# A first stage with the modulation weights ahead of x, and two stage ends interleaved with half output blocks

## The reference, cut to what matters

```python
def first_block(x, c, ctx, c_ctx, ada_w, ...):            # x (1,512,1024), ctx (1,256,1024)
    sh_l, sc_l, gt_l = adaln(c, ada_w[0], ada_b[0])        # silu(c) @ w + b, split in three
    h_lat = rms_norm(x, norm_g[0]) * (1 + sc_l) + sh_l
    h_ctx = rms_norm(ctx, norm_g[0]) * (1 + sc_c) + sh_c   # the same with c_ctx
    y_lat = hgrn_mixer(h_ctx, h_lat, ...)                  # 5 projections a head, scan, norm, gate, @ hg_w_out
    x = x + gt_l * y_lat
    h = rms_norm(x, norm_g[1]) * (1 + sc) + sh
    u, z = split(h @ ft_w_in, 2)
    y = real(fft2(u in 8 groups of 256 channels)) * silu(z)
    x = x + gt * (y @ ft_w_out)
    return rms_norm(x, final_g)
```

## Time and profile before

| | |
|---|---|
| three runs | 2678.82, 2682.83, 2678.87 us |
| the profiled execution | 2684.97 us, of it the span from first to last instruction 2683.3 us |
| PE matmul busy | 2537.6 us, 95% |
| DVE, ACT, POOL busy | 1622.8 (60%), 1002.2 (37%), 113.7 us (4%) |
| mean granted clock of PE | 0.978 of full |
| DMA | 223.82 MB, mean 83 GB/s |
| one cut of a block | `w_hi` on ACT 1.06 us (line 847), `w_lo` on DVE 1.22 us (line 1324), means |
| ACT, 128x512 from PSUM | 0.60 us (line 937) |

### The profile page before, as it was taken

How to read it: one execution, slowest core, us unless ns; L and a number is a source line. 1 busy time by engine, 2 the same in 40 slices (tenths; PEclk the granted TensorE clock), 3 DMA queues, 4 the chain that set the end, 5 groups by cost and what they waited for, 6 DMA issues and landing times.

```text
span 2683.3 us, 40458 instructions
## 1 busy us (share of the span) xinstructions
PE 2537.6 (95%) x14516; PEld 2181.5 (81%) x14516; DVE 1622.8 (60%) x2366; ACT 1002.2 (37%) x1350; POOL 113.7 (4%) x140
## 2 busy tenths in 40 slices
PE   6999999999999998999899999989999899999996
PEld 1788888888888776888789999978888667888885
DVE  5567777777777645444455343468999755544445
ACT  3334444444344323333244222245545443322222
POOL 0011211121111000000000000000000000000000
PEclk9999999999999998999899999989999899999998
DMA  5122221221122222222122222222222212222222
GB/s 225 63 71 66 74 71 63 70 78 63 63 70 78 86 87 69 73 70 74 60 86 94 86 94 87 93 79 89 95 92 86 77 63 86 94 94 94 94 94 86
DMA packets 59817, 223.82 MB, mean 83 GB/s; under 512 B 6496, under 2 KB 6496, under 8 KB 59264
## 3 DMA queue, kind: packets, MB, share of 16 engines
q1 hardware_dynamic: 56544, 207.94, 23.3%
q0 software_dynamic: 3232, 15.34, 1.6%
HBM read 221.15 MB, written 2.10 MB: 83 GB/s over the span
## 4 chain that ended last, share of the span: by engine, by line
PE 85%; DVE 6%; ACT 4%; issue 3%; DMA 1%; DVEq 0%; ACTq 0%; SPq 0%; POOL 0%
PE ps L441 74%; PE ps L600 4%; PE ps L622 1%; PE ps L498 1%; DVE w_lo L1324 1%; DVE cv L1927 1%; ACT L942 1%; DMA ada_raw<-in_ada_weights_dram 1%; PE ps L641 1%; PE ps L613 1%; PE ps L632 1%; PE ps L587 1%; PE ps L634 1%; PE ps L633 1%; ACT w_hi L847 0%
## 5 line engine op out<-in xcount | busy, mean ns | idle before, releaser
L847 ACT ACTIVATE w_hi<-w_raw 128x1024 fp32r<-128x1024 f32 x360 | 381.4, 1060 | 1003.7 <-PE ps L441 998.0
L1324 DVE TENSOR_TENSOR w_lo<-w_raw,w_hi 128x1024 fp32r<-128x1024 f32 x360 | 439.7, 1222 | 256.6 <-ACT w_hi L847 254.7
L441 PE MATMUL ps<-n_hi,w_hi 128*128 128x512 f32 (+1 forms) x992 | 323.9, 358 | 30.1 <-DVE w_lo L1324 16.4
L441 PE MATMUL ps<-n_hi,w_lo 128*128 128x512 f32 (+1 forms) x992 | 320.6, 355 | 0.0
L441 PE MATMUL ps<-n_lo,w_hi 128*128 128x512 f32 (+1 forms) x992 | 320.4, 355 | 0.0
L441 PE MATMUL ps<-h_hi,w_hi 128*128 128x512 f32 x640 | 273.6, 428 | 8.4 <-DVE h_lo L1351 4.2
L441 PE MATMUL ps<-h_hi,w_lo 128*128 128x512 f32 x640 | 255.3, 399 | 0.0
L441 PE MATMUL ps<-h_lo,w_hi 128*128 128x512 f32 x640 | 254.8, 398 | 0.0
L441 PEld LDWEIGHTS ps<-n_hi,w_hi 128*128 128x128 f32 x992 | 175.0, 190 | 66.5 <-issue 21.5
L441 PEld LDWEIGHTS ps<-n_lo,w_hi 128*128 128x128 f32 x992 | 176.4, 191 | 27.2 <-issue 0.2
L441 PEld LDWEIGHTS ps<-n_hi,w_lo 128*128 128x128 f32 x992 | 175.7, 190 | 26.6
(11 more groups left out here) (338 smaller groups left out, 5075.5 us busy)
## 6 DMA issues: line engine op xcount, KB each, us to landing
w_raw<-in_weights_dram SPq DMA_DIRECT2D x376, 512.0 KB, 3.3
ada_raw<-in_ada_weights_dram SPq DMA_DIRECT2D x4, 2048.0 KB, 25.8
gate_raw<-in_gate_weights_dram POOLq DMA_DIRECT2D x16, 512.0 KB, 3.6
x<-in_x_dram SPq DMA_DIRECT2D x1, 2048.0 KB, 11.1
x<-in_x_dram POOLq DMA_DIRECT2D x1, 2048.0 KB, 7.8
out_dram<-fin POOLq DMA_DIRECT2D x1, 2048.0 KB, 6.5
xc<-in_ctx_dram POOLq DMA_DIRECT2D x1, 1024.0 KB, 11.2
masks<-in_masks_dram POOLq DMA_DIRECT2D x1, 512.0 KB, 13.4
```

The costliest lines, as they stand in the source:

```text
L441: last = nc.tensor.matmul(o, w, xp, start=start and n == 0, stop=stop and n == 2)
L847: run(w_hi[:, s], w_raw[:, s], ACT.Copy).then_inc(hi_ready[s], 1)
L1324: tt(w_lo[:, s], w_raw[:, s], w_hi[:, s].bitcast(F32), ALU.subtract).then_inc(lo_ready[s], 1)
```

## The change

Three parts of the program change.

1. First stage. SP loads modulation part 0 ahead of x, and ctx after part 1; POOL issues identity after ctx has landed and the masks after part 3 has. The squares go through two buffers. The context mean is taken on PE right after modulation part 1, into bank 5. ACT rather than DVE copies the modulation rows. DVE divides x and ctx by their roots in place (`over_root`) while PE still works on the modulation; afterwards ACT makes `h_hi` straight from the divided x with scale and bias, and DVE makes a temporary and `h_lo` beside it (`first_lo`).
2. Last head. All eight half blocks of the first four outputs are taken inside the pass, in 16 parts, at every place where a projection part stood and two after the norm. The four later half blocks leave out the tiles of the last two heads (`LATE` = 2), whose weights ACT and DVE keep aside (`kept_hi`, `kept_lo`). After the pass PE adds these two heads to the four banks. DVE's four residual additions then read banks at `early_done`.
3. Last Fourier group. The stream's order is changed (`OUT_ORDER`) so that four first halves of the output come before four second halves. The first halves run between the steps of group 7, the second halves after it, with waits on the last two y tiles alone. `residual(RF)` runs the last four rows; `raw_residual` is written out rather than looped, also for its second user.

```diff
-            sp.dma_start(x0[:], x_in).then_inc(x_in_s, 16)
             for n, (dst, a, b_) in enumerate(ADA_LOADS):
                 sp.dma_start(dst, ada_in[a:b_].rearrange("b p n -> p b n")).then_inc(ada_loaded[n], 16)
-            with sp.Fori(0, nblocks // 2) as i:
+                if n == 0:
+                    sp.dma_start(x0[:], x_in).then_inc(x_in_s, 16)
+                elif n == 1:
+                    sp.dma_start(xc[:], ctx_in).then_inc(xc_in_s, 16)
+            with sp.Fori(0, BLOCKS_TO_OUT // 2) as i:
...
-            pool.dma_start(xc[:], ctx_in).then_inc(xc_in_s, 16)
+            pool.wait_ge(xc_in_s, 16)
+            pool.dma_start(ident[:], ident_in).then_inc(ident_in_s, 16)
+            pool.wait_ge(ada_loaded[3], 16)
             pool.dma_start(masks[:], mask_in).then_inc(const_in_s, 16)
-            pool.dma_start(ident[:], ident_in).then_inc(ident_in_s, 16)
...
             for n, (raw_, a, b_) in enumerate(ADA_LOADS):
-                if n == 3:
-                    mean(N0, T, st_sum[:, 0])
                 pe.wait_ge(ada_loaded[n], 16)
                 for k in range(KD):
+                    if n == 1 and k == KD - 2:
+                        mean(N0, T, st_sum[:, 0])
...
+                if n == 1:
+                    mean(N0C, TC, st_sum[:, 1], bank=5)
...
+                parts = iter([(k, n) for k in range(2 * EARLY) for n in range(2)])
+                def begin_output():
+                    k, n = next(parts)
+                    xs = as_cut({"lo": y_cut}, whole(y_hi, y_lo))
+                    if n == 0:
                         s = take(k)
                         pe.wait_ge(acc_free, HEADS * 6 + 2)
+                    at, half = k // EARLY * KD, (KD - (LATE if k >= EARLY else 0)) // 2
+                    last = tiles(k % 2, [ps[:, k % EARLY]], xs, range(at + half * n, at + half * (n + 1)),
+                                 k < EARLY and n == 0, False, half * n)
...
+            pe.wait_ge(kept_s, EARLY)
+            for n in range(LATE):
+                t = HEADS - LATE + n
+                pe.wait_ge(y_cut, t + 1)
+                for k in range(EARLY):
+                    last = three([ps[:, k]], kept_hi[:, k, n * P:(n + 1) * P], kept_lo[:, k, n * P:(n + 1) * P],
+                                 [y_hi[:, t]], [y_lo[:, t]], False, n == LATE - 1)
+                    if n == LATE - 1:
+                        last.then_inc(early_done, 1)
...
-                project(0); turn(); project(1); over_tokens(0); over_tokens(1)
-                project(2); over_channels(0); project(3); over_channels(1)
+                project(0); turn(); project(1); begin_output(0); over_tokens(0); begin_output(1); over_tokens(1)
+                project(2); begin_output(2); over_channels(0); project(3); begin_output(3); over_channels(1)
...
-            residual(RF, KD // 2, 2, whole(y_hi, y_lo), T)
+            st.enter(0, EARLY)
+            for k in range(EARLY):
+                s = take(k)
+                tiles(s, [ps[:, k]], last_y, range(KD, 2 * KD), False, True).then_inc(w_used[s], 1)
+            st.leave(1)
+            residual(RF, (KD - EARLY) // 2, 2, whole(y_hi, y_lo), T, done=EARLY)
...
+            def over_root(N, x, rt_):
+                dve.wait_ge(N["root"], 1)
+                own.link(v.reciprocal(rt_, rt_))
+                for k in range(KD):
+                    tt(x[:, k], x[:, k], rt_, ALU.mult).then_inc(N["tmp"], 1)
+            over_root(N0, x0, st_sq[:])
             cut(0)
             cut(1)
+            over_root(N0C, xc, st_tmpc[:, 2])
...
+            def first_lo(N, x, n, tmp, hi, lo):
+                for k in range(KD + 1):
+                    if k < KD:
+                        if k > 1:
+                            dve.wait_ge(N["lo"], k - 1)
+                        own.mark(ts(tmp(k), x[:, k], scale[:, n, k:k + 1], ada0[:, k, n:n + 1], ALU.mult, ALU.add))
+                    if k:
+                        own.wait(1 if k < KD else 0)
+                        dve.wait_ge(N["hi"], k)
+                        tt(lo(k - 1), tmp(k - 1), hi(k - 1).bitcast(F32), ALU.subtract).then_inc(N["lo"], 1)
...
+                def early_after(k):
+                    if i is not None:
+                        return
+                    if EARLY <= k + 2 < 2 * EARLY:
+                        s, use = st.slot(k + 2)
+                        dve.wait_ge(kept_s, k + 3 - EARLY)
+                        tt(kept_lo[:, k + 2 - EARLY], w_raw[:, s, BLK - LATE * P:BLK],
+                           kept_hi[:, k + 2 - EARLY].bitcast(F32), ALU.subtract)
+                    cut(k + 2)
```

More of the change, by code:

```diff
@@ L53 @@
 Z_BANK = 2
+BLOCKS_TO_OUT = HEADS * 6 + 2 * KD + 4 * GROUPS
+OUT_ORDER = [BLOCKS_TO_OUT + 2 * m + n for n in range(2) for m in range(EARLY)]
+LATE = 2
 EPS = 1e-6
@@ L201, in program @@
         h_hi, h_lo = h.take("h_hi", [P, KD, T], F32R), h.take("h_lo", [P, KD, T], F32R)
+        kept = h.over()
+        kept_hi, kept_lo = [kept.take(f"kept_{n}", [P, EARLY, LATE * P], F32R) for n in ("hi", "lo")]
         hc_hi, hc_lo = h.take("hc_hi", [P, KD, TC], F32R), h.take("hc_lo", [P, KD, TC], F32R)
@@ L479, in mean @@
                 else:
-                    last = nc.tensor.matmul(ps[:, 6, 0:n], ones_d[:], src[:, 0:n], start=True, stop=True)
+                    last = nc.tensor.matmul(ps[:, bank, 0:n], ones_d[:], src[:, 0:n], start=True, stop=True)
                 last.then_inc(N["mean"], 1)
@@ L506, in _ @@
             last.then_inc(ada_done, 1)
-            pe.wait_ge(N0["root"], 1)
-            mean(N0C, TC, st_sum[:, 1])
+            pe.wait_ge(N0C["root"], 1)
             def tile(t):
@@ L913, in dve @@
                     act.wait_ge(dve_scan, j * DVE_SCAN + n)
+                def early_after(k):
+                    if i is not None or j is None:
+                        return
+                    st.wait_done(act, k)
+                    if EARLY <= k + 2 < 2 * EARLY:
+                        s, use = st.slot(k + 2)
+                        act.wait_ge(w_loaded[s], use * 16 + 16)
+                        run(kept_hi[:, k + 2 - EARLY], w_raw[:, s, BLK - LATE * P:BLK], ACT.Copy).then_inc(kept_s, 1)
+                    cut(k + 2)
                 def refill(k):
                     if i is None:
-                        if j is not None and k < EARLY:
-                            after(k)
-                    elif k == 3:
+                        return
+                    if k == 3:
                         s, _ = st.slot(5)
@@ L1136, in _, with raw_residual @@
             st.leave(GROUPS - 1)
+            st.enter(0, EARLY)
             act_group(None, GROUPS - 1)
[L1139 to L1152, removed]
+            st.leave(1)
+            def raw_residual(R, N, blocks, src, hi, gain, sq):
+                st.enter(0, sum(blocks))
+                done = 0
+                for m_, nb in enumerate(blocks):
+                    for k in range(done, done + nb):
+                        after(k)
+                    done += nb
+                    act.wait_ge(R["res"], m_ + 3)
+                    run(hi(m_), src(m_), ACT.Identity, bias=zero[:], scale=gain(m_)).then_inc(N["hi"], 1)
+                    act.wait_ge(R["add"], m_ + 1)
+                    run(sq, src(m_), ACT.Square).then_inc(R["sq"], 1)
+                st.leave(1)
             act.wait_ge(meta_scaled, 1)
             run(xg_hi[:, :, 0:META], meta_g[:], ACT.Copy).then_inc(meta_hi, 1)
-            raw_residual(RF, NF1, KD // 2, 2, lambda m_: row(x1, m_), lambda m_: row(xg_hi, m_)[:, META:TM],
+            raw_residual(RF, NF1, (1,) * EARLY + (2,) * (KD - EARLY), lambda m_: row(x1, m_),
+                         lambda m_: row(xg_hi, m_)[:, META:TM],
                          lambda m_: fgain[:, ds(m_, 1)], n1["sq"][:, 0])
@@ L1334, in sum_squares, with norm_apply @@
                         dve.wait_ge(R["add"], k)
[L1335 removed]
+                        tt(acc, acc, sq(k), ALU.add).then_inc(R["add"], 1)
                     else:
[L1337 to L1343 removed]
+                        v.tensor_copy(acc, sq(k)).then_inc(R["add"], 1)
+            def norm_apply(N, src, gain, shift, tmp, rt_, hi, lo):
+                dve.wait_ge(N["root"], 1)
+                own.link(v.reciprocal(rt_, rt_))
                 for k in range(KD + 1):
@@ L1761, in dve_group @@
                 next_block(1)
+                if i is None:
+                    after(0)
                 fold(1)
```

215 lines of the change are left out of this document (124 added, 91 removed).

## The result

The changed kernel takes 2658.4 us (median of 4 runs, 2657.03 to 2658.74) against 2680.85 of the kernel before beside it: a ratio of 0.9915, 95% interval 0.9897 to 0.9932. Faster, as forecast, but by 22 us and not by 36, and 3.4 us above the forecast's range. Span and clock of the profiled executions: 2656.8 us at 0.980 after, 2683.3 at 0.978 before.

A forecast was written before the change was run, and what follows sets the result against it. PE carries 85% of the chain of waits, so time is won only where PE waits or runs at the lower clock. 18 + 6.5 + 11.1 = 35.6 us off 2678.87 gives 2643.3; range 2635 to 2655.

The forecast's parts named there:

- First stage: Earlier modulation and projections, faster tiles and fewer PE waits there win 18 us, bounds 12 to 20.
- Landing of part 0: First stage: the first modulation weights land at 8.7 us, no later than 12.4, where x landed before.
- Tile pace: First stage: DVE takes about 1.05 us a tile instead of 1.45, so eight tiles win 1.9 us.
- Rival (a): First stage bound by landings and DVE's division chain: gain 12 there, time 2649; chance 0.12.
- Last head: Output parts fill PE's gaps in the last head up to the norm: net gain 6.5 us, bounds 0 to 10.
- the bunched residual: After the last head, DVE's four residual additions come together: PE waits 3.1 us, then loses about 2 to lower clock.
- Rival (b): Last head gives nothing: DVE's cuts precede merges PE awaits, and the bunched residual returns the rest; time 2650, chance 0.10.
- Last Fourier group: Half blocks of output cover PE's waits in the last group: gain 11.1 us, bounds 5 to 13.
- The 4.22: Last Fourier group: PE's 4.22 us wait ahead of `turn`, for group 6's last y, stays.
- the other case that the prediction worked out: Last Fourier group: transposes do not count as busy, the first half block pays the whole clock ramp; 0.4 us less gain.
- Rival (c): Fourier part does little, as each `after` delays the group's own chain by a whole half block: gain 5, time 2649; chance 0.04.
- Rival (d): Slower: PE's new phase leaves it at 1.2 GHz in the steady heads; 100 us there would give 2693; chance 0.03.

The follow-up runs named there:

- e1: Changed kernel with 32 tiny DVE memsets ahead of the token mixer's loop, which then starts at 869; 2647.81 us.
- e4: Kernel before with 58 tiny DVE memsets ahead of the mixer's loop, which then starts at 838 as in the changed kernel; 2693.45 us.
- e14: Kernel before with 53 DVE memsets ahead of the mixer's loop, which then starts at 833; 2691.10 us.
- e8: Changed kernel, loop at 870, DVE's four additions moved ahead of weight cuts and last-residual preparation ahead of the meta tokens' landing; 2642.25 us.
- e2: Changed kernel with 64 tiny DVE memsets ahead of the mixer's loop, which then starts at 901; 2648.48 us.
- e3: Changed kernel with 96 tiny DVE memsets ahead of the mixer's loop, which then starts at 933; 2645.28 us.
- e12: Kernel before with 40 DVE memsets ahead of the mixer's loop, which then starts at 820; 2681.59 us.
- e13: Kernel before with 48 DVE memsets ahead of the mixer's loop, which then starts at 828; 2682.79 us.

## Why the prediction was wrong, point by point

**The step that failed** is this one: "Splitting SP's loop, writing out `raw_residual` and dropping unused semaphores cost nothing: SP's queue issues far ahead of need, and DVE waits on PE in those loops." It costed the instructions where they run. It did not ask what they do to the code behind them. The sum has no term for that. The change adds 57 instructions to DVE's program, 29 of them in the first stage and 24 in the last group, `raw_residual` among these, and so moved the mixer's loop from 781 to 838, into the 13 bad places. The writing out that the step names would not have done it alone. Price: 10.6 us by e1 against the changed kernel, 12.8 by e4, 9.6 by e14. By the two traces PE waits 6.5 us more at the three back edges and loses about 4 to the lower clock behind the first and the third. DVE had no slack there: the weights that it cuts first after the jump are those for which PE waited up to 1.6 us already. No other step is needed for the miss: with e1's loop the time is 2647.8, inside the range of 2635 to 2655.

**First stage**, 18 forecast, 16.9 measured. Landing of part 0: 8.7 taken, 9.72 measured, between the bounds of 9.0 less overlap and 12.4; the landing at 12.4 that the prediction held against it did not come. The sum took 12 passes at 18.8; they began at 19.66. Last pass at 41.2, was 42.3. `over_root` was to be hidden with 1 us in hand: it was, with the 1.19 of idle time in the row at 44.21. First projection at 44.8, was 46.59. Tile pace 1.05, was 1.18, since the temporary took 0.55 and not 0.42: I had scaled a row of 768 columns down by its width, which gives too little. Third block 61.5, was 63.54, and without the wait, as said. Rival (a) fell.

**Last head**, 6.5 forecast, 8.4 measured. The wait ahead of `output` 0.8, was 0.69; the last y 1, was 0.88; the bunched residual 3.1 and 2 of lower clock, was 2.46 with about six matmuls at 0.43 for 0.23, 1.2 us. That it can be had cheaper e8 shows. Rival (b) fell.

**Last Fourier group**, 11.1 forecast, 10.3 measured. The 4.22 stays to the hundredth. Lower clock at the start of the first half block: 1.3 taken, since the transposes were to use up part of it; PE went from them into the half block without a wait and still ran nine matmuls at the lower level (1251.83 to 1255.82), about 1.8 us, so the other case that the prediction worked out, 0.4 less gain, is the one that came. The wait that comes late next was named with its cause (the preparations behind `meta`): 0.9, was 1.11. Rival (c) fell.

**The clock.** Rival (d) fell: the mean is 0.980 for 0.978.

**The base.** The forecast subtracts from 2678.87; the kernel before ran at 2680.85 beside the changed one, which is 2 us of the 15.1 between 2643.3 and 2658.4. 10.6 are the loop's place by e1 (9.9 and 13.1 by e2 and e3). The other 2.5 are within what one set of runs can tell.

## What to carry to other kernels

A change that adds instructions to an engine moves every loop behind them. For a long loop (270 instructions here) count where it starts, before and after, and look in the timeline at its back edge: "issue" ahead of its first instruction, and more packets of the instruction queue than before. Where a change gains less than its parts, lay the two traces beside each other at marks from the start on; the first mark at which the lead shrinks names the place, even if nothing was changed there. A few idle instructions ahead of such a loop are a repair for it, 5 of them were enough here, and 40 or 48 cost nothing that the runs can tell (e12, e13).

## What the runs showed of the hardware

A jump back in DVE's program costs 0.5 us when the loop of 270 instructions starts at 781, 820, 828, or 842 to 933, and 3.0 when it starts at 833, 838 or 1094. With three such jumps the instruction queue moves 31 to 34 packets of 8 KB in the whole execution in place of 16 or 17: five more for each (31 for 16). In a row of equal short instructions a gap of 0.33 to 0.36 us comes every 128. A TENSOR_SCALAR of 128x512 with a factor and an addend per partition takes 0.55 us, a TENSOR_TENSOR of the same size 0.69.
